# State-space output of a two-layer block built as tokens by features

## The reference

```
proj = h @ w_in[i]
z, xbc, dt_raw, q, k, v = jnp.split(proj, splits, axis=-1)
...
cb = jnp.einsum("bclgn,bcsgn->bgcls", Cc, Bc)                  # per group of 4 heads
y_diag = jnp.einsum("bgcls,bgrcls,bcsgrp->bclgrp", cb, lmat, X)  # X = xh * dt
...
y = (y_diag + y_off).reshape(b, s, H, P) + xh * d_skip.astype(jnp.float32)[:, None]
y = y.reshape(b, s, SSD_WIDTH) * jax.nn.silu(z.astype(jnp.float32))
yg = y.reshape(b, s, G, SSD_WIDTH // G)
yg = yg * lax.rsqrt(jnp.mean(yg * yg, axis=-1, keepdims=True) + EPS)
y = yg.reshape(b, s, SSD_WIDTH) * norm_w.astype(jnp.float32)
...
y_att = dilated_attention(q, k, v).reshape(b, s, ATT_WIDTH)
x = x + jnp.concatenate([y_ssd, y_att], axis=-1) @ w_out[i]
```

## Time and profile before

| | us |
|---|---|
| median of 3 runs | 1887.58 (1887.3 to 1887.69) |
| the profiled execution | 1887.55 |
| its span | 1885.8 |
| TensorE busy | 1878.2, 11164 matmul records |
| VectorE, ScalarE, GpSimd busy | 1451.7, 1170.4, 397.5 |
| granted clock of TensorE | 1.00 |

### The profile page before, as it was taken

The page is one execution under the profiler, slowest core; times in us unless marked ns, Lnnn a source line. Parts: engine busy times, 40 slices in busy tenths (PEclk is TensorE's granted clock), DMA queues, the critical chain, the costliest instruction groups (busy, mean ns, idle before and its releaser), DMA issues.

```text
span 1885.8 us, 29598 instructions
## 1 busy us (share of the span) xinstructions
PE 1878.2 (100%) x11164; PEld 1628.2 (86%) x11164; DVE 1451.7 (77%) x2607; ACT 1170.4 (62%) x2165; POOL 397.5 (21%) x456
## 2 busy tenths in 40 slices
PE   9999999999999999999999999999999999999999
PEld 8889988897898888888988788888888898878887
DVE  6877996677799769866787978757885687897874
ACT  6667785567678556545667565545554667756552
POOL 2210211011011005411022214402440102223430
PEclk9999999999999999999999999999999999999999
DMA  9344566543465656665554355555555544445553
GB/s 354 124 141 145 194 204 204 173 152 123 136 196 192 206 170 205 190 195 180 179 167 136 124 189 190 190 191 186 192 190 191 189 158 153 150 145 185 189 193 127
DMA packets 92333, 334.62 MB, mean 177 GB/s; under 512 B 10240, under 2 KB 10784, under 8 KB 91808
## 3 DMA queue, kind: packets, MB, share of 16 engines
q1 hardware_dynamic: 92192, 332.73, 53.6%
HBM read 331.61 MB, written 1.08 MB: 176 GB/s over the span
## 4 chain that ended last, share of the span: by engine, by line
PE 91%; DVE 6%; ACT 2%; issue 1%; DVEq 0%; ACTq 0%
PE PS L83 88%; PE PS L86 3%; DVE WL L98 2%; DVE TMP L98 1%; DVE TMP L108 1%; DVE TMP L105 1%; ACT TMP L95 1%; ACT WH L92 1%; DVE SM L114 1%; DVE M L108 0%; DVE SM L108 0%; ACT TMP L92 0%; ACT M L92 0%; ACT TMP L94 0%; DVE SM L105 0%
## 5 line engine op out<-in xcount | busy, mean ns | idle before, releaser
L98 DVE TENSOR_TENSOR WL<-RAW,WH 128x1024 fp32r<-128x1024 f32 (+1 forms) x610 | 760.1, 1251 | 281.5 <-ACT WH L92 277.8
L92 ACT ACTIVATE WH<-RAW 128x1024 fp32r<-128x1024 f32 (+1 forms) x610 | 640.1, 1053 | 310.0 <-PE PS L83 305.3
L83 PE MATMUL PS<-WH,GX 128*128 128x512 f32 (+1 forms) x1636 | 524.7, 392 | 0.0
L83 PE MATMUL PS<-HX,WH 128*128 128x512 f32 (+1 forms) x1920 | 523.5, 344 | 0.4
L83 PE MATMUL PS<-HX,WL 128*128 128x256 f32 x1488 | 413.9, 281 | 0.0
L83 PE MATMUL PS<-GX,WH 128*128 128x256 f32 (+1 forms) x1776 | 409.6, 330 | 0.4
L83 PEld LDWEIGHTS PS<-HX,WH 128*128 128x128 f32 x1920 | 331.1, 189 | 46.6 <-DVE TMP L108 0.8
L83 PEld LDWEIGHTS PS<-WH,GX 128*128 128x128 f32 x1636 | 306.2, 188 | 64.6 <-issue 3.7
L83 PEld LDWEIGHTS PS<-GX,WH 128*128 128x128 f32 x1776 | 298.0, 190 | 30.2 <-DVE TMP L108 0.8
L83 PE MATMUL PS<-WL,GX 128*128 128x512 f32 (+1 forms) x818 | 317.1, 388 | 0.0
L98 POOL TENSOR_TENSOR TMP<-TMP,RB 128x256 f32<-128x256 f32 x176 | 205.6, 1172 | 473.5 <-DVE TMP L98 235.1
(11 more groups left out here) (146 smaller groups left out, 1679.4 us busy)
## 6 DMA issues: line engine op xcount, KB each, us to landing
RAW<-wts SPq DMA_DIRECT2D x607, 512.0 KB, 4.3
CUM<-rows SPq DMA_DIRECT2D x8, 512.0 KB, 4.9
M<-bias SPq DMA_DIRECT2D x4, 320.0 KB, 11.7
M<-bias SPq DMA_DIRECT2D x1, 1280.0 KB, 8.8
X<-x SPq DMA_DIRECT2D x2, 512.0 KB, 10.9
M<-mem SPq DMA_DIRECT2D x1, 1024.0 KB, 13.0
M<-memt SPq DMA_DIRECT2D x1, 1024.0 KB, 11.4
CST<-cst SPq DMA_DIRECT2D x1, 794.0 KB, 12.6
```

Of the source, the lines that this page charges most:

```text
L83: return Issued(self.eng and self.eng.matmul(o, l, r, start=first, stop=last, skip_group_check=share))
L92: return Issued(self.eng.activation(o, i, f, scale=scale))
L98: return Issued(self.eng and self.eng.tensor_tensor(o, a, b, op))
```

## The change

- z is computed by `tm_wide` with 512 columns, tokens by features: two halves of 8 steps instead of 8 tiles. tanh and gate work on 512 columns.
- In `y_pair` the decays are held still (three blocks of 128 x 128) and XD moves with 64 columns, so y comes out tokens by features, in two banks for a group. D becomes a row of 16 values and is multiplied to x when X is turned back; the skip only adds.
- ScalarE sums the squares while it squares. The inverse root is then a column for each token, and `y_normed` multiplies by it; `y_sums` and `y_scale` go. `y_turn` transposes the normed result back, four transposes for a group, and high and low part are taken from the bank, times the norm weight.
- The last two gatings move from GpSimd to VectorE.
- The rates are written anew, and with them the places of the fillers, of "xd" and of "cb".
- The host lays out the z weights by token order.

```diff
-        DIL_RATES = [1, 1, 1] + [1, 1, 0] * 3 + [0, 1, 0] * 5
-        PREP_RATES = [0, 0, 0] + [0, 1, 0] + [1, 1, 0] + [0, 0, 0] + [1, 0, 0] * 5
-        DIL_PARTS = [0, 0, 0] + [2, 2, 1] + [1, 1, 0] * 2 + [0, 1, 0] * 5
+        DIL_RATES = [1, 1, 1] + [1, 1, 0] * 2 + [1, 2, 0] + [1, 1, 0] * 5
+        PREP_RATES = [0, 0, 0] + [0, 1, 0] + [1, 1, 0] + [0, 0, 0] + [1, 0, 0] + [1, 1, 0] * 2 + [0, 0, 0] * 2
+        DIL_PARTS = [0, 0, 0] + [2, 2, 1] + [1, 1, 0] + [1, 2, 0] + [1, 1, 0] * 5
...
-        SSD_RATE = 1.5
+        SSD_RATES = [2.5] + [1.5] * 7
...
-                    for m in range(8):
-                        fm_tile(("z", L, m), whole, WT if m >= 2 else (0, 1))
-                        yield
+                    for c in range(2):
+                        yield from tm_wide(("z", L, c), whole, 512, (0, 1) if c == 0 else (2, 7))
...
-                def y_sums(g):
-                    if g % 2 == 0:
-                        take(("ys", L, g // 2), (3, 6))
-                    ps = bank(("ys", L, g // 2))
-                    for q in range(2):
-                        m_ = 2 * g + q
-                        e.wait_ge(squared, ("y", L, m_))
+                def y_pair(p):
+                    g = p // 2
+                    if p % 2 == 0:
                         for t in range(2):
-                            m = e.mm(ps[:, t * 2 + g % 2:t * 2 + g % 2 + 1],
-                                     y_sq(m_)[:, t * 128:t * 128 + 128], cc(C_ONE, 1),
-                                     g % 2 == 0 and q == 0 and t == 0, q == 1, share=True)
-                    m.then_inc(summed, ("y", L, g))
-                def y_scale(g):
-                    e.wait_ge(small, ("ry", L, g // 2))
-                    put_over(("ry", L, g), [RY[:, t * 4 + g:t * 4 + g + 1].to_broadcast([128, 128])
-                                            for t in range(2)], (4, 5))
-                def y_pair(p):
-                    ob = take(("y", L, p), (3, 6))
+                            take(("y", L, g, t), ((3, 6), (4, 5))[g % 2])
                     e.wait_ge(dout, ("xd", L, 3))
-                    os = [ob[64 * u:64 * u + 64, 0:256] for u in range(2)]
-                    for u in range(2):
-                        h = 2 * p + u
+                    for h in (2 * p, 2 * p + 1):
                         e.wait_ge(made, ("mask", L, h))
-                        e.mm(os[u], XD[:, 0, h * 64:h * 64 + 64], dec_t(h)[:, 0:256], True, False)
-                    for u in range(2):
-                        h = 2 * p + u
-                        m = e.mm(os[u][:, 128:256], XD[:, 1, h * 64:h * 64 + 64], dec_t(h)[:, 256:384], False, True)
+                        o0, o1 = (bank(("y", L, g, t))[:, h % 4 * 64:h % 4 * 64 + 64] for t in range(2))
+                        x0, x1 = (XD[:, t, h * 64:h * 64 + 64] for t in range(2))
+                        e.mm(o0, dec_t(h)[:, 0:128], x0, True, True)
+                        e.mm(o1, dec_t(h)[:, 128:256], x0, True, False)
+                        m = e.mm(o1, dec_t(h)[:, 256:384], x1, False, True)
                     m.then_inc(weighed, ("y", L, p))
...
+                def y_turn(g):
+                    ps = take(("yt", L, g), ((3,), (6,), (4,), (5,))[g])
+                    e.wait_ge(made, ("yn", L, g))
+                    for i in range(4):
+                        t, f = i % 2, i // 2
+                        m = e.turn(ps[:, i * 128:i * 128 + 128], y_tokens(2 * g + t)[:, f * 128:f * 128 + 128], ident)
+                    m.then_inc(turned, ("yt", L, g))
...
+                fill.beat(2)
+                for p in range(8):
+                    fill.beat(SSD_RATES[p])
+                    y_pair(p)
                 fill.beat(1)
-                for p in range(8):
-                    fill.beat(SSD_RATE)
-                    if p == 6:
-                        y_sums(1)
-                    y_pair(p)
-                    if p == 5:
-                        y_sums(0)
-                fill.beat(1)
-                y_sums(2)
-                y_scale(0)
-                y_scale(1)
-                fill.beat(1)
-                y_sums(3)
+                y_turn(0)
+                y_turn(1)
                 fill.rest()
...
                 def y_square(m):
-                    e.wait_ge(gated, ("yz", L, m))
-                    if m >= 4:
-                        e.wait_ge(summed, ("y", L, m // 2 - 2))
-                    e.act(ACT.Square, y_sq(m), XC[:, m, :]).then_inc(squared, ("y", L, m))
+                    if m < 6:
+                        e.wait_ge(gated, ("yz", L, m))
+                    else:
+                        e.wait_ge(made, ("yz", L, m))
+                    e.wait_ge(squared)
+                    g, t = m // 2, m % 2
+                    e.act(ACT.Square, y_sq(m), y_tokens(m), acc=SUMY[:, t, g:g + 1]).then_inc(squared, ("y", L, m))
...
                 def yk_high(m):
-                    e.wait_ge(made, ("yn", L, m))
-                    e.act(ACT.Copy, GH[:, 8 + m, :], yn_t(m)).then_inc(ahi, ("yk", L, m))
-                fill.beat(1)
+                    e.wait_ge(turned, ("yt", L, m // 2))
+                    e.act(ACT.Copy, GH[:, 8 + m, :], bank(("yt", L, m // 2))[:, m % 2 * 256:m % 2 * 256 + 256],
+                          scale=col(pb + Q_SN + m)).then_inc(ahi, ("yk", L, m))
...
-                def z_end(m):
-                    key = ("z", L, m)
-                    e.wait_ge(scored, (("dil", L), 2 * m + 1))
-                    e.wait_ge(ready, ("zt", L, m))
-                    e.stt(Z[:, m, :], band_t(m), 1.0, bank(key)[:, 0:S], ALU.add, ALU.mult).then_inc(dout, key)
+                def z_end(c):
+                    e.wait_ge(scored, (("dil", L), 8 * c + 7))
+                    for t in range(2):
+                        key = ("z", L, c), t
+                        e.wait_ge(ready, ("zt", L, c, t))
+                        e.stt(gate_block(c, t), zt_t(2 * c + t), 1.0, bank(key)[:, :], ALU.add, ALU.mult).then_inc(dout, key)
                 def others():
                     for i in range(KD):
                         lows((("v2", L, 1), i))
                         yield
-                    for m in range(8):
-                        lows(("z", L, m))
-                        if 2 <= m < 7:
-                            z_end(m - 2)
-                        if m >= 6:
-                            z_end(m - 1)
+                    for c in range(2):
+                        for i in range(KD):
+                            lows((("z", L, c), i))
+                            if c == 1 and i == 1:
+                                z_end(0)
+                            yield
+                    for i, _ in enumerate(residual(("wa", L), 8, behind=True, hold=True)):
+                        if i == 0:
+                            z_end(1)
                         yield
-                    z_end(7)
-                    yield from residual(("wa", L), 8, behind=True, hold=True)
...
-                            m = e.tt(dst, ps[:, t * 256:t * 256 + 256].rearrange("p (h d) -> p h d", h=4), by, ALU.mult)
-                        m.then_inc(dout, key)
+                            e.tt(dst, ps[:, t * 256:t * 256 + 256].rearrange("p (h d) -> p h d", h=4), by, ALU.mult)
+                        by = PAR[:, pb + Q_D + 4 * b:pb + Q_D + 4 * b + 4].unsqueeze(1).unsqueeze(3).to_broadcast(
+                            [128, 2, 4, 64])
+                        e.tt(M[:, b * 512:b * 512 + 512].rearrange("p (t h d) -> p t h d", t=2, h=4),
+                             ps[:, :].rearrange("p (t h d) -> p t h d", t=2, h=4), by, ALU.mult).then_inc(dout, key)
...
-                def y_skip(m):
-                    y = XC[:, m, :]
-                    e.wait_ge(weighed, ("y", L, m))
-                    e.stt(y, y, col(pb + Q_D + m), bank(("y", L, m))[:, 0:256], ALU.mult, ALU.add).then_inc(
-                        dout, ("y", L, m))
+                def y_skip(g):
+                    e.wait_ge(weighed, ("y", L, 2 * g + 1))
+                    for t in range(2):
+                        y, key = y_tokens(2 * g + t), ("y", L, g, t)
+                        e.tt(y, y, bank(key)[:, 0:256], ALU.add).then_inc(dout, key)
+                def y_gated(m):
+                    e.wait_ge(dout)
+                    e.tt(y_tokens(m), y_tokens(m), y_gate(m), ALU.mult).then_inc(made, ("yz", L, m))
                 def y_norm(i):
-                    e.wait_ge(summed, ("y", L, 2 * i + 1))
+                    e.wait_ge(squared, ("y", L, 4 * i + 3))
                     e.wait_ge(small)
-                    e.ts(smc(0, 4), bank(("ys", L, i))[:, 0:4], 1.0 / 1024, EPS, ALU.mult, ALU.add).then_inc(dout, ("ys", L, i))
-                    e.wait_ge(dout)
+                    v = smc(0, 4).rearrange("p (t g) -> p t g", t=2)
+                    e.ts(v, SUMY[:, :, 2 * i:2 * i + 2], 1.0 / 1024, EPS, ALU.mult, ALU.add).then_inc(small)
                     y = newton(4).rearrange("p (t g) -> p t g", t=2)
```

(56 more changed lines are left out.)

81 lines of the change are left out of this document (43 added, 38 removed).

## The result

The changed kernel takes 1915.4 us (median of 4 runs, 1915.02 to 1919.5), the kernel before 1887.47 in the same runs; the ratio is 1.0153 (95% interval 1.0142 to 1.0165), so 27.9 us slower. The forecast was 1907, range 1890 to 1913: the direction and most of the size were right, and the range ended 2.4 us too low. The profiled execution has a span of 1913.5, 27.7 more than before.

A forecast was written before the change was run, and what follows sets the result against it. TensorE bounds the kernel, busy 1878.2 of 1885.8 us. Per layer, work and old waits -2.5, moved products and small waits +10.5, stage end +2.0; twice that is +20 on 1887.6, told as 1907 us, range 1890 to 1913.

The forecast's parts named there:

- TensorE's own work: Per layer: z steps gain 1.3 us, state-space products cost 2.8 more, dropped sums and scales against new transposes give -2.6.
- waits of before that go: State-space stage: old TensorE waits for banks, VectorE's skip and ScalarE vanish, 1.4 us a layer, between 0.24 and 1.8.
- two second products: Attention iterations 5 and 6: second B x C waits 3.8 us for bank 7, together +7.6 a layer.
- first product of iteration 5: Attention: B x C waits for bank 7 behind X's three multiplications and a WL, +1.2 us a layer, between 0 and 2.
- first step of z: It waits for two banks held by X blocks with a third multiplication, +0.6 us a layer, between 0 and 1.4.
- last iteration, copy: Last attention iteration: transposes wait for exponentials and scaling, ScalarE's copy for two tanh; +1.1 us, between 0 and 1.5.
- last transposes: End of the state-space stage: TensorE waits for VectorE's longer path (13.9 against 11.9), +2.0 us a layer, between 0 and 3.5.
- rival 3: State-space products: the 64 moving columns are not hidden behind weight loads, +5 us a layer, 1917; chance 4%.
- TensorE's clock falls in the new waits: After 4 waits of 3.8 us TensorE runs slower, 4 to 14 us more, 1911 to 1921; chance 12%.
- rivals 2 and 3: TensorE's clock falling in the new waits (12%, 1911 to 1921), and 64 moving columns not hidden behind loads (4%, 1917).
- rival 1: Attention: the bank waits don't come about and work alone decides, 1883 to 1887 or 1880; chance 18%.
- second estimate: VectorE's normings run two results a cycle: tail about 0.8 us shorter, 1.2 of wait, the whole 1.6 less.

The follow-up runs named there:

- kernel kept busy: Changed kernel with matmuls that nothing reads put ahead of the second products B x C and of group 2's transposes back; 1908.16 us, ratio 1.011.
- kernel with three edits: Changed kernel with B x C spread over iterations 4 to 6 and two banks, taken ahead of WL on VectorE, last transposes one step later; 1887.79 us.

## Why the prediction was nearly right, and where it failed

**The forecast as a sum.** Per layer, forecast and measured in the profiled execution:

| | forecast | measured |
|---|---|---|
| TensorE's own work | -1.1 | -1.2 |
| waits of before that go | -1.4 | -0.4 |
| two second products | 7.6 | 7.2 |
| first product of iteration 5 | 1.2 | 0.2 |
| first step of z | 0.6 | 0.3 |
| weighings, waiting for the low part | not seen | 1.7 |
| last iteration, copy | 1.1 | 0.2 |
| last transposes | 2.0 | 2.2 |
| clock | 0 | 3.6 |

The waits measured come to 11.85 a layer (23.7 / 2), against 12.5. The work follows by subtraction: 1913.5 - 23.7 - 7.2 (clock, by the kernel kept busy) = 1882.6, and before 1885.8 - 0.8 = 1885.0. The kernel with three edits, which has no slow stretch, gives 1886.0 - 5.1 = 1880.9; so the work is 1.2 to 2.0 a layer shorter. Such subtractions between single executions are no better than that, for the kernel's start alone differs by 0.8: its second group of matmuls starts at 7.62 us before and at 6.78 in the changed kernel.

**Right:** the new limit and its place. Two products back to back on VectorE behind a WL, on one bank, make TensorE wait, and the filler between the transposes makes it long. The walk through three engines' rows had it within 0.2 us (3.8 against 3.64, 3.61, 3.64 and 3.59). Some of that closeness is luck, since both ends of the wait came late, its start by 0.5 and its end by 0.3. The runs with another bank, another order on VectorE and another place of the filler each took away the link they were meant to. The price of a pair (1.25, rival 3 out) and VectorE's tail were right as well.

**Off in size, without much effect:** three small waits were put at 2.9 together and came to 0.7; the weighings, which I did not have (the bank of the output is free only after VectorE's low part, queued between two RECIPROCALs that wait for the exponentials; that these come later now is my reading, and the run with the low part ahead of the RECIPROCALs bears only a part of it out), came to 1.7. They roughly cancel, which is luck. The waits that went with the change were 0.4, not 1.4: only what the rows showed was there, and the rest that I added from "short stretches" had no row.

**Wrong:** the step "TensorE's clock falls in the new waits" was left out of the forecast as a rival with 12%, and the range left it out too. It happened, at the price I gave it (4 to 14; measured 7.2), in four places: behind three of the four waits of 3.6 and behind one of the two at the last transposes, which the rival didn't have. With a clock term of 7 the forecast would have been 1914. The evidence in the trace was one-sided: TensorE had stood still for over a microsecond only at the start, and there it was slow afterwards. In the rest it never stood still that long, so the clock of 1.00 there said nothing about a wait of 3.6. I took a missing case for evidence against. The rows at the start were also a weak price: the same 16 passes took 6.75 before and take 5.21 in the changed kernel, while the granted clock in the rows is 1.00 there in both, so only the pace shows the slowness.

```profile
1.22 5.21 PE L83 MATMUL PS<-SQ 128*128 128x256 f32 x16 [1.22 <-DVE SQ L126]
```

The Trainium skill (TensorE: Matmul & The Clock Gate, What's actually happening) states that the low clock is the default and activity lifts it. The trace agrees, by the rows of low clock behind four of six long waits and by the 1.000 of the kernel kept at work.

The range failed with it. It was meant for 8 in 10, but rivals 2 and 3, which had 16% together, lay mostly above 1913, and rival 1 with 18% below 1890; by these chances it held little more than the 66% of the forecast as told.

**The smaller rule.** For the normings the prediction had a second estimate, a tail 0.8 shorter. The Trainium skill (VectorE: DVE Perf Modes, Mode 2×_2P) states that an operation with a single source in SBUF gives two results a cycle even in fp32. The trace agrees in the direction, not in the size. Four normings take 1.05 (1094.85 to 1095.90), 0.26 each, where I took 0.33 and the second estimate came to 0.20 (0.8 less for six); the two gatings next to them, with two sources, take 0.34 each (1088.88 to 1089.56). So an operation of this kind is cheaper, by about half of what that estimate gave, and the tail came out 0.4 shorter than mine.

**Where the change's gain went.** Work saved on TensorE is 2.4 to 4.1 us in all. Its order of the products, the tail and the later low parts cost 22.9 of new waits, and the clock behind them 7.2. With the waits mended the gain is given back to what is left of them (5.1 in the kernel with three edits), and the result is no difference. Whether the layout itself could win if these last waits went is open; no run shows it.

## What to carry to other kernels

When an operation moves in the order of an engine, count from a fixed point (here the end of the scores) when its resource is asked for and when it is free, link by link over all engines; that gave 3.8 where 3.6 was measured. Then price each new wait of the bound engine twice: the wait, and the slower clock behind it, which here made 27.9 out of 20.7. And a range holds no more of the chance than the rivals outside it leave. A bank that is asked for again in the same iteration wants a second bank, or its reader ahead of anything that waits for another engine.

## What the runs showed of the hardware that was not expected

- The low clock behind a wait is not a fixed price. Waits of 3.64 were followed by a mean clock of 0.52 over 7 us in one layer and by 1.00 in the other; waits of 2.2 before the last transposes by 0.66 in one and full speed in the other. Behind the four waits of 1.58 (the product ahead of the WL) the mean stayed 1.00, and behind a wait of 1.56 (another bank, second layer) it was 0.66 over 5 us. So the length of the wait alone doesn't decide it; what does, no run shows.
- It can begin after TensorE has taken up work again. At 1648.00 the products still run at full pace and the slow stretch starts some 1.7 us later (the scores take 1.59 instead of 0.86):

```profile
1648.00 0.92 PE L83 MATMUL PS<-M 128*128 128x256 f32 x4 [3.59 <-DVE M L98]
1648.85 0.97 PE L83 MATMUL PS<-TMP,M 128*64 128x256 f32 x8
1649.75 1.66 PE L83 MATMUL PS<-M 64*128 64x128 f32 x8
```

- Matmuls that nothing reads, put into a wait, cost nothing and kept the clock at its upper level: 7.2 us less with 40 more of them.
